# One-hot quads in bf16 over 22 expert groups, the mixed input finished by quarters, and POOL's rounding as a copy

## The reference, cut to what matters

```python
# end of the first block
e = rms_norm(p[i] @ w_ple_proj[i], ple_norm_gain[i])
x = x + jax.nn.sigmoid(x @ w_ple_gate[i]) * e
...
# start of the second: n feeds c_q (384), c_kv (256), k_pe (64) and the rest
n = rmsnorm(h, norm_mix[l])
parts = jnp.split(n @ w_in[l], offsets, axis=-1)
...
# PEER: idx in 0..16383, gate = softmax of the best scores
act = jax.nn.gelu(jnp.einsum('bpd,bphkd->bphk', hb, u).astype(jnp.float32), approximate=False)
coef = (act * gb).astype(hb.dtype)
return jnp.einsum('bphk,bphkd->bpd', coef, v_tab[ib])
```

## Time and profile before

| | |
|---|---|
| median of the runs | 2790.92 us (2785.6 to 2791.35) |
| profiled execution | 2792.14 us, its span 2790.4 us |
| PE busy | 2638.9 us, 95% |
| DVE, ACT, POOL busy | 1310.3, 909.4, 769.8 us |
| mean granted clock of PE | 0.97 |

### The profile page before, as it was taken

How to read it: one execution, slowest core, us unless ns; L and a number is a source line. 1 busy time by engine, 2 the same in 40 slices (tenths; PEclk the granted TensorE clock), 3 DMA queues, 4 the chain that set the end, 5 groups by cost and what they waited for, 6 DMA issues and landing times.

```text
span 2790.4 us, 29980 instructions
## 1 busy us (share of the span) xinstructions
PE 2638.9 (95%) x12275; PEld 1598.8 (57%) x12416; DVE 1310.3 (47%) x2249; ACT 909.4 (33%) x1088; POOL 769.8 (28%) x606
## 2 busy tenths in 40 slices
PE   6998988899998889988899999999999999999999
PEld 5776665456776667767344666666444444444444
DVE  6364231412256622249974676767124454443443
ACT  3133422831233331021233545454332322322321
POOL 7674551314241339867664000000000000000000
PEclk9999988998999999999999999999999999999999
DMA  4222221101011112311433444544725555455451
GB/s 165 85 76 76 76 68 57 53 23 62 31 46 46 46 46 95 131 62 58 161 143 137 166 181 167 217 190 181 308 114 211 197 196 223 184 208 214 181 218 53
DMA packets 71432, 359.41 MB, mean 129 GB/s; under 512 B 5488, under 2 KB 38640, under 8 KB 45312
## 3 DMA queue, kind: packets, MB, share of 16 engines
q1 hardware_dynamic: 71296, 357.48, 34.7%
HBM read 286.16 MB, written 71.30 MB: 128 GB/s over the span
## 4 chain that ended last, share of the span: by engine, by line
PE 86%; DVE 7%; ACT 2%; issue 2%; POOL 2%; DMA 0%; SPq 0%; DVEq 0%; ACTq 0%; POOLq 0%
PE ps L696 8%; PE ps L1201 8%; PE ps L1203 8%; PE ps L1202 8%; PE ps L697 8%; PE ps L698 8%; PE ps L1152 8%; PE ps L1151 8%; PE ps L1150 8%; PE ps L1175 4%; PE ps L685 2%; PE ps L1055 2%; PE ps L778 1%; DVE area L2062 1%; PE ps L969 1%
## 5 line engine op out<-in xcount | busy, mean ns | idle before, releaser
L2210 POOL TENSOR_TENSOR wring_parts<-wring,cst 128x512 fp32r<-128x512 f32 (+1 forms) x253 | 291.1, 1181 | 648.2 <-PE ps L698 483.7
L1151 PE MATMUL ps<-sqbuf,wring 128*128 128x512 bf16 x998 | 380.0, 381 | 8.5 <-POOL wring L2235 7.1
L1152 PE MATMUL ps<-sqbuf,wring 128*128 128x512 bf16 x998 | 379.9, 381 | 1.4
L1150 PE MATMUL ps<-sqbuf,wring 128*128 128x512 bf16 x997 | 379.4, 381 | 1.6 <-POOL wring L2235 0.3
L2215 POOL TENSOR_TENSOR wring_parts<-wring,wring_parts 128x512 fp32r<-128x512 f32 (+1 forms) x253 | 341.2, 1378 | 5.3
L2154 DVE TENSOR_TENSOR area<-area 128x4096 bf16<-128x4096 f32 x32 | 141.5, 4425 | 338.6 <-ACT area L1614 338.6
L1614 ACT ACTIVATE area<-area 128x4096 bf16<-128x4096 f32 x32 | 115.6, 3616 | 453.8 <-PE ps L1203 453.8
L696 PE MATMUL ps<-resid_parts,wring_parts 128*128 128x512 f32 (+3 forms) x584 | 229.4, 394 | 8.0 <-DVE normed_x_parts L1715 6.9
L697 PE MATMUL ps<-normed_x_parts,wring_parts 128*128 128x512 f32 (+3 forms) x584 | 226.2, 388 | 0.0
L698 PE MATMUL ps<-resid_parts,wring_parts 128*128 128x512 f32 (+3 forms) x584 | 224.4, 386 | 0.0
L1598 ACT ACTIVATE area<-ps 128x512 f32<-128x512 f32 x128 | 76.3, 597 | 443.1 <-PE ps L1152 443.0
(11 more groups left out here) (236 smaller groups left out, 4571.5 us busy)
## 6 DMA issues: line engine op xcount, KB each, us to landing
wring<-in_weights_dram SPq DMA_DIRECT2D x66, 1024.0 KB, 4.8
area<-in_vT_dram SPq DMA_DIRECT2D x32, 2048.0 KB, 7.8
wring<-in_uT_dram SPq DMA_DIRECT2D x16, 2048.0 KB, 7.7
area<-in_uT_dram SPq DMA_DIRECT2D x16, 2048.0 KB, 9.5
hidden_table<-area SPq DMA_DIRECT2D x32, 1024.0 KB, 4.2
gate_table<-area SPq DMA_DIRECT2D x8, 4096.0 KB, 19.2
normed_x<-gate_table SPq DMA_DIRECT2D x32, 1024.0 KB, 10.4
rt<-hidden_table SPq DMA_DIRECT2D x16, 1024.0 KB, 10.9
```

What stands on the lines that cost most here:

```text
L1150: pe.matmul(out, u_hi[:, k, n], h_hi[:, k, :], start=(k == 0), stop=False)
L1151: pe.matmul(out, u_hi[:, k, n], h_lo[:, k, :], start=False, stop=False)
L1152: mm = pe.matmul(out, u_lo[:, k, n], h_hi[:, k, :], start=False, stop=(k == KD - 1))
L2210: ins = nc.gpsimd.tensor_tensor(up[:, d, :], W(name)[:, d, :], C("ones", 0, 1).unsqueeze(1).to_broadcast([P, step, n]), ALU.mult)
```

## The change

**One-hots in bf16.** Both one-hot matrices are written as bf16. The gate is no longer multiplied into the first but into the second, as a high and a low bf16 part (w_hi, w_lo), side by side: 256 columns. ACT makes them with six activations of 128x128 a quad, each with a scale pointer; DVE makes the low parts of tokens 2 and 3. PE multiplies four times 128x256 in bf16, into two PSUM banks. DVE adds the two halves with a reduce over the innermost axis of two, straight into the stage tile; ACT's copy goes away. A quad may now be spread when the reduce of the quad two before is done (four before, until now).

```diff
-BEFORE, BESIDE = 8, 16
+BEFORE, BESIDE = 8, 22
 QUADS = T // 4
-QUADS_A_GROUP = QUADS // BESIDE
+def quads_of(g):
+    n = g - BEFORE
+    return range(QUADS * n // BESIDE, QUADS * (n + 1) // BESIDE) if 0 <= n < BESIDE else range(0)
...
+        def spread_out(n):
+            at = 4 + 2 * (n % 2)
+            return ps[:, at:at + 2, :].rearrange("p b (t n) -> p (b t) n", t=2)
...
             def spread_quad(n):
                 q = n % 4
                 pe.wait_ge(hot, n + 1)
-                pe.wait_ge(hot_n2, n + 1)
-                if n >= 4:
-                    pe.wait_ge(copied, n - 3)
+                pe.wait_ge(hot_gates, n + 1)
+                if n >= 2:
+                    pe.wait_ge(copied, n - 1)
                 for j in range(4):
-                    mm = pe.matmul(ps[:, 4 + q, j * P:(j + 1) * P], oneA[:, 4 * q + j, :], oneB[:, 4 * q + j, :],
-                                   start=True, stop=True)
+                    mm = pe.matmul(spread_out(n)[:, j, :], oneA[:, q, j, :],
+                                   gateB[:, q, j, :, :].rearrange("p z n -> p (z n)"), start=True, stop=True)
                 mm.then_inc(spread, 1)
...
-            def copy_quad(n):
...
+            def weigh_gates(n):
+                q = n % 4
+                act.wait_ge(hot_second, n + 1)
+                if n >= 4:
+                    act.wait_ge(spread, n - 3)
+                for i in range(4):
+                    t = 4 * n + i
+                    ins = act.activation(gateB[:, q, i, 0, :], oneB[:, q, i, :], ACT.Copy, scale=entT[:, 2, t:t + 1])
+                    if i < 2:
+                        act.activation(gateB[:, q, i, 1, :], oneB[:, q, i, :], ACT.Copy, scale=w_lo[:, t:t + 1])
+                ins.then_inc(hot_gates, 1)
...
+                dve.tensor_tensor(oneB[:, q], iota, across(1), ALU.is_equal).then_inc(hot_second, 1)
+                dve.tensor_tensor(oneA[:, q], iota, across(0), ALU.is_equal)
+                dve.wait_ge(hot_second, n + 1)
+                dve.tensor_tensor(gateB[:, q, 2:4, 1, :], oneB[:, q, 2:4, :],
+                                  w_lo[:, 4 * n + 2:4 * n + 4].unsqueeze(2).to_broadcast([P, 2, P]), ALU.mult
+                                  ).then_inc(hot, 1)
+            def add_quad(n):
...
+                dve.wait_ge(spread, n + 1)
+                dve.tensor_reduce(dst[:, 4 * i:4 * i + 4, :], out.rearrange("p t (z n) -> p t n z", z=2), AX_X, ALU.add
+                                  ).then_inc(copied, 1)
```

```diff
-            for n in range(QUADS):
-                one_hots(n)
-                g = BEFORE + n // QUADS_A_GROUP
-                if n % QUADS_A_GROUP == 1 and g > BEFORE:
-                    split_u(g + 1)
+            for g in range(BEFORE, BEFORE + BESIDE):
+                for i, n in enumerate(quads_of(g)):
+                    if n + 2 < QUADS:
+                        one_hots(n + 2)
+                    add_quad(n)
+                    if i < 4 and BEFORE < g < GROUPS - 1:
+                        split_u(g + 1, i)
...
-                if g == BEFORE + BESIDE:
+                if g == BEFORE + BESIDE - 1:
                     sp.wait_ge(stored[0], 8 * PIECES)
                     load_v(0)
```

```diff
-            big_sums("mix", TM)
-            project_h(("cq", 0), ready=KD)
-            project_h(("cq", 1))
-            project_h(("ckv", 0), TM, meta_first=True)
+            big_sums("mix", TM, (0, 1, 2))
+            latent_query(0, (0,))
+            big_sums("mix", TM, (3,))
+            latent_query(0, (1, 2, 3))
+            latent_query(1, range(4))
+            project_h(("ckv", 0), TM, ready=KD, meta_first=True)
+            sums("cq", ones, [[0, T, 2 * T]])
...
                 dve.tensor_tensor(x, x, sg, ALU.add).then_inc(x2_ready, 1)
-            dve.wait_ge(x2_ready, 4)
-            split_norm(1, "mix", "mix", TM)
+                dve.wait_ge(x2_ready, m + 1)
+                gain(m, xs, "mix", x2_gained)
+                split_gained(1, m, X2_PARTS, x2_gained)
+            split_norm(1, "mix", "mix", TM, {3: lambda: scale_latent(0), 6: lambda: scale_latent(1)})
```

```diff
-                    ins = nc.gpsimd.tensor_tensor(up[:, d, :], W(name)[:, d, :],
-                                                  C("ones", 0, 1).unsqueeze(1).to_broadcast([P, step, n]), ALU.mult)
+                    ins = nc.gpsimd.tensor_copy(up[:, d, :], W(name)[:, d, :])
```

More of the change, by code:

```diff
@@ L325, in build @@
         mixedT = view(0, KD, T)
+        x2_gained = view(0, KD, T)
         eT = view(4096, KD, T)
@@ L780, in sums, with big_sums @@
                 fills(mm, key)
-            def big_sums(name, width=T):
+            def big_sums(name, width=T, pairs=range(4)):
                 key = ("ss", name)
-                claim(key)
+                if pairs[0] == 0:
+                    claim(key)
                 sq = norm_sq(name)[:, 0:KD * width].rearrange("p (k t) -> p k t", k=KD)
-                for m in range(4):
+                for m in pairs:
                     pe.wait_ge(squares, 4 * BIG.index(name) + m + 1)
@@ L942, in _ @@
                 project_part(name)
+                if n == 0:
+                    sums("kpe", heads64, [[0]], TM)
                 if n >= 1:
                     sum_part(PARTS[n - 1])
+                if n == 1:
+                    rotate_key()
                 if n >= 3 and PARTS[n - 3][0:2] == "qp":
@@ L1216, in _ @@
             for g in range(BEFORE, BEFORE + BESIDE):
-                first = QUADS_A_GROUP * (g - BEFORE)
-                pre(g, range(first, first + QUADS_A_GROUP))
+                pre(g, quads_of(g))
             for g in range(BEFORE + BESIDE, GROUPS):
@@ L1378, in _ @@
                 copy_out(("pg", m), sgT[:, 2 * m:2 * m + 2, :], pair(("pg", m)), ACT.Sigmoid)
-            for m in range(4):
                 act.wait_ge(x2_ready, m + 1)
                 square_two("mix", m, resid[:, 2 * m:2 * m + 2, :], TM)
+                round_gained(1, m, X2_PARTS, x2_gained)
             root("mix", TM)
@@ L1598, in gelu @@
                 act.activation(hid_out[g % 2][:, j, :], ps[:, j, :], ACT.Gelu).then_inc(gelu_done, 1)
-            def copy_quad(n):
-                piece, i = n // (QUADS // PIECES), n % (QUADS // PIECES)
-                if i == 0 and piece >= 2:
-                    act.wait_ge(stored[piece % 2], 16 * (piece // 2))
-                dst = stage[:, piece % 2, :].rearrange("p (j t) -> p t j", t=HALF)
-                act.wait_ge(spread, n + 1)
-                act.activation(dst[:, 4 * i:4 * i + 4, :], ps[:, 4 + n % 4, :].rearrange("p (t j) -> p t j", t=4),
-                               ACT.Copy).then_inc(copied, 1)
+            def weigh_gates(n):
[9 more added lines that the diff above has]
+                ins.then_inc(hot_gates, 1)
             def round_v(g):
@@ L1633, in _ @@
                                ).then_inc(turned_copied, 1)
+            act.wait_ge(turned_copied, TT)
+            act.activation(w_hi, entT[:, 2, :], ACT.Copy).then_inc(gates_rounded, 1)
+            act.wait_ge(gates_split, 1)
+            weigh_gates(0)
+            weigh_gates(1)
             for g in range(BEFORE, BEFORE + BESIDE):
-                first = QUADS_A_GROUP * (g - BEFORE)
                 for j in range(EG):
                     gelu(g, j)
-                    copy_quad(first + 2 * j)
-                    copy_quad(first + 2 * j + 1)
-                round_u(g + 2)
+                    for n in quads_of(g)[2 * j:2 * j + 2]:
+                        if n + 2 < QUADS:
+                            weigh_gates(n + 2)
+                if g + 2 < GROUPS:
+                    round_u(g + 2)
             for g in range(BEFORE + BESIDE, GROUPS):
@@ L1707, in _, with split_norm @@
                                           ALU.add, ALU.subtract))
-            def split_norm(turn, name, gain, width):
+            def split_norm(turn, name, gain, width, between={}):
                 r = inverse(name, width)
@@ L1723, in split_norm @@
                         lower(k - 1)
+                    if k in between:
+                        between[k]()
                 lower(KD - 1)
@@ L1864, in rope @@
                 dve.tensor_tensor(dst, dst, tmp, ALU.add).then_inc(roped, 1)
-            rope(0, ("rot", "kpe"), kp, flat(("rot", "kpe"))[:, MF], C("cos"), C("sin"), rot_tmp[:, 0:TM])
             def part(name):
@@ L1884, in _ @@
             copy_part(PARTS[0])
+            rope(0, ("rot", "kpe"), kp, flat(("rot", "kpe"))[:, MF], C("cos"), C("sin"), rot_tmp[:, 0:TM])
             for n, name in enumerate(PARTS):
```

161 lines of the change are left out of this document (103 added, 58 removed).

## The result

The changed kernel takes 2711.38 us (median of 4 runs, 2709.66 to 2713.37), the kernel before 2789.78 (over all four of its runs). The ratio is 0.9721, 95% interval 0.9705 to 0.9738: 78 us faster, where 65 were forecast. The span of the profiled execution is 2709.9 us.

The account below looks back on a forecast made before the run. PE was taken as the bound, busy 95% of 2790.4 us. One-hots with 22 groups -36, mixed input -26 and POOL's copy -3 sum to -65: 2790.9 to 2726 us, range 2708 to 2775.

Parts of the forecast that it names:

- One-hot quads and 22 groups: One-hot stage up to the combine: cheaper bf16 quads -53.8 us, new waits +10, spreading over 22 groups +8, together -36 us.
- the first rival: One-hot stage: the reduce's hops at every element make DVE the bound, reduce 1.85 us, total 2765 to 2785 us; 17%.
- the slower case: One-hot stage: a reduce of 2.1 us and more makes the kernel slower than before, 2785 to 2815 us; 8%.
- the bursts: One-hot stage: quads come in pairs, so PE waits 0.3 to 0.5 us for the fourth reduce in 18 groups, about +8.
- The mixed input: Gate projections' end to first query part: 64 us against 93.2, so -29, +3.2 for moved work: -26, between -20 and -31.
- rival four: Beside the gate projections DVE and POOL block each other; pg2 and pg3 wait 2 to 4 us each, total -55 to -58; no chance given.
- the wait at ckv0: Before the first query part: POOL can split ckv0's weights only when cq0 frees the slot, priced at 4 us of PE wait.
- The clock's 5 us: Gate projections' end to first query part: 5 us allowed for lower clock, within the 64 us forecast for that stretch.
- POOL's copy: POOL's weight splits: a copy of 0.75 us for the product, paying only where PE waits for POOL: -3, between -9 and +2.
- the +3 of new contention: Beside pg1 to pg3: POOL's new company with DVE costs up to +3 us, set against the copy's gains.
- ACT as the bound: One-hot stage: six weighings in a row at 0.394 us delay gelu and hidden blocks' banks, +5 to +15; no chance given.
- the walk: One-hot stage: one group of six quads followed in order; fourth reduce ends at 18.2 us, PE wants it at 17.9.

## Why the prediction was right

**One-hot quads and 22 groups: right, -36 forecast.** From the turning to the combine the traces give -34.8, and +1.9 behind it. The reduce took 1221 ns, where I had taken 1.22 from the plain reduces and kept 2.2 for the hop at each element. So the first rival and the slower case, which rest on the hop, fall by that one row. Two misses nearly cancel. The matmuls gave more than I had counted: a pair of quads takes 0.88 us from its start to that of the next matmul (1571.83 to 1572.71), so a quad 0.44 and not 0.47, and 128 x (0.89 - 0.44) is 57.6 us for 53.8; nothing is left of the fixed part that I had allowed for. The waits took more: 13.0 for 8 at the bursts, 8.7 at the start (6.4 before, +2 to 3 forecast), and 7.4 ahead of the combine for 6. In the last the size came out right by luck: DVE's two subtractions for v were missing from the sum, and the tables arrived earlier than I had them.

**The mixed input: the mechanism right, -26 forecast.** Alone it measured 26. That figure holds errors that cancel. The stretch is 31.5 us shorter where I had said 29. What is moved behind the first query parts does not cost 3.2: the stretch from "part" to the first matmul of L761 (at 559.2 us in the kernel before), which takes in what was moved, goes from 81.9 to 82.8 us. Against both stand the 3.1 us of rival four, which I had left out of this term: -31.5 + 0.9 + 3.1 = -27.5. In the full kernel the stretch is 34.5 us shorter. The term that was off is the wait at ckv0: 4 forecast; the wait of 1.6 us left in the list is for the normalised parts. The clock's 5 us were too many too, at 0.97. The chain of the changed kernel shows how it runs:

```profile
...
376.40 6.39 PE ps L813 x24
385.68 2.08 PE ps L813 x8
388.11 1.28 ACT L1303
...
392.10 0.78 DVE normed_x L1776
...
396.94 1.13 DVE area L1910
...
406.58 1.71 DVE normed_x_parts L1772
...
```

The sums of three quarters start with the end of the gate projections (376.40), the last sum at 385.68, ACT's root at 388.11, and DVE's normalising from 392.10 on, with the scaling of cq0 (L1910) between. The price of some of DVE's operations there is 1.7 us in place of 0.7, beside POOL's splits.

**POOL's copy: the direction right, the size wrong.** -3 was forecast, measured -10 alone and some -18 in the changed kernel. The duration was right (0.75 taken, 0.742 measured). The step that failed is "10.6 belong to the gap of the top-k at 1297 which DVE's chain sets", by which nothing was counted there; "query" to "group 0" is 6.4 us shorter. DVE's chain does set most of that gap, but POOL's product held this chain up by 5.3 us, and POOL's split stood without idle time between DVE's last step and PE. The start gave 7.3 us (384.3 to 377.0) where I had 2 + 1.4, and -2 for all contention, and the +3 of new contention beside the gate projections came only with the product. Beside POOL's product four small operations of DVE took 4.04 us where they took 0.49 in a gap of POOL. The Trainium skill ("SBUF — State Buffer", Who interferes with whom) says that DVE, in a mode that uses both its port pairs or with two SBUF inputs, contends with GpSimd, and that the one to issue first holds the shared ports for its whole instruction while the other blocks. The trace agrees in size, as each of the four took about as long as one product (1.01 us); whether they run in such a mode no run here shows.

**The sum.** -65 was forecast and -78 measured, so the range held, but the 13 us between them aren't spread evenly. By the traces the one-hots with 22 groups gave 33 for 36, the stretch of the mixed input 34.5 for 26, and the start and the top-k's gap, which only the copy can shorten, 7.9 + 6.4 = 14 for 3. The total is near because the largest two terms were.

**The rivals.** ACT as the bound didn't come: its activations start 0.295 us apart, it is busy 68% of the stage, and no wait of PE for the gelus (L1642) stands in the list. The Trainium skill's rule on hops ("Vector Engine (DVE) Microarchitecture Reference", 5.2) did not apply in its general form; its exception, one source alternating between two regions with one word written for two read, is what this case's 1221 ns agrees with, here out of PSUM and with the halves 512 bytes apart.

## What to carry to other kernels

An engine off the critical path must be judged by the instants in which it is the last, and by what it does to the engine that is on the path: a cheaper operation on POOL, busy 28% of the time, gave three to six times what I had counted, since I had handed its longest wait to DVE, whose chain POOL itself was lengthening. Where two engines feed a third in bursts, a walk through one period in program order tells the waits better than the sum of busy time (0.72 and 1.52 us, where the sum predicts none and the walk 0.3 to 0.5 for the first). When a stage's end moves closer to its consumer, list everything that stands in the queues between, in order: reordering DVE's two subtractions was worth 9.3 us, as much as spreading over one group less (7.5).

## What the runs showed of the hardware that I had not expected

A reduce that takes its two addends from places 128 words apart in PSUM, and writes with a stride of 64 words into SBUF, costs 1221 ns for 1024 elements, just as the reduce of contiguous elements in SBUF does (1216 ns). ACT's copy with the same strided write took 1075 ns for 512 where its gelu of 512, written densely, takes 598. POOL's copy of 128x512 to the rounded type takes 0.57 us undisturbed (2.28 us for four, in the kernel with the copy), where the product with ones takes 1.01 (4.04 for four). Four operations of DVE on 64 elements a partition take 0.49 us while POOL is idle and 4.04 us beside four of POOL's products.
